# Moving attention's value products to the end of a unit, with a second pair of buffers for the turned weights

## The chip, the cores and the metric

The kernel runs on one NeuronCore of one Trainium2 chip, as one launch. The metric is the device time of that core in microseconds (us), as the median of several executions; smaller is better. The names of the engines are those of the profile: PE is TensorE's matmul, PEld its weight load, DVE is VectorE, ACT is ScalarE, POOL is GpSimd, SP is SyncE.

## The reference, cut to what matters

The reference is one inference step of a two-layer streaming encoder: 512 frames of a new stream (the prompt) and 32 next frames of a running stream (the sample) with 512 cached frames. Each layer projects the frames, runs three gated branches (convolution, spatial gating, stick-breaking attention), merges them, and ends with a feed-forward part. All in fp32. The change touches the attention alone:

```python
SB_HEADS = 8
SB_HEAD_DIM = BRANCH_W // SB_HEADS      # 64
SB_QBLOCK = 128

def stick_breaking(q, k, v, q_pos, k_pos):
    z = jnp.einsum('bqhd,bkhd->bhqk', q, k, preferred_element_type=jnp.float32) * (SB_HEAD_DIM ** -0.5)
    mask = k_pos[None, :] < q_pos[:, None]
    log_keep = jnp.where(mask, jax.nn.log_sigmoid(-z), 0.0)
    later = lax.cumsum(log_keep, axis=3, reverse=True) - log_keep
    attn = jnp.where(mask, jnp.exp(jax.nn.log_sigmoid(z) + later), 0.0)
    return jnp.einsum('bhqk,bkhd->bqhd', attn.astype(v.dtype), v)

def stick_breaking_prompt(q, k, v):
    outs = []
    for i in range(seq // SB_QBLOCK):
        lo, hi = i * SB_QBLOCK, (i + 1) * SB_QBLOCK
        outs.append(stick_breaking(q[:, lo:hi], k[:, :hi], v[:, :hi], pos[lo:hi], pos[:hi]))
    return jnp.concatenate(outs, axis=1)
```

So a block of 128 queries sees one to four blocks of 128 keys: its weights are 128, 256, 384 or 512 wide.

## The kernel before, in words

**The big products.** Nearly all of the time is TensorE multiplying fp32 weights that ScalarE and VectorE split into a high and a low part (`wh`, `wl`); each product takes three matmuls of 272 columns (`three`, L1563, L1568, L1569). A chunk of weights (`chunk`) serves four units (`unit`): a unit fills one PSUM bank `acc` with 8 x 3 = 24 matmuls. `chunk` calls `mid(b)` after the first 12 matmuls of unit b and `end(b)` after the last.

**Attention rides in these gaps.** In five chunks of each layer (20 units, u = 0 to 19) TensorE does attention's small matmuls in the middle of unit u (`within(u)`) and at its end (`behind(u)`). Attention comes in 18 steps. Steps 0 to 15 are for the prompt: step n has heads 2(n/4) and 2(n/4)+1 and query block n%4, so its weights are (n%4+1) x 128 wide. Steps 16 and 17 are for the sample. One step passes through the engines like this:

- `scores(n)` on TensorE, at the end of unit n, for both heads, into the banks `score0` and `score1` (L1637);
- `sigmoids(n)` on ScalarE, called from `before(n+1)`: `keep` and `beta` of each head from the scores (L528, L529; odd steps keep their `beta` in `gex`);
- masks on GpSimd (L449), two selections per head;
- `made(n)` on VectorE, called from `attend(n+1)`: a scan (L1047) and a product (L1050) per head;
- `turns(n, 0)` on TensorE in the middle of unit n+2 and `turns(n, 1)` at its end: the weights of head 0 and of head 1 are transposed into the one bank `turned` (L1664), and ScalarE copies each out of it into `att` (L546, in `turned`);
- `values(n)` on TensorE in the middle of unit n+3, ahead of `turns(n+1, 0)`: the products with `vtok` (L1685) for both heads into the one bank `small`;
- `out_rows(n)` on ScalarE (L560, from `within(n+3)`) copies the result's high part out of `small`, and `rows_lo(n)` on VectorE (L1073, from `attend(n+3)`) takes the low part. It raises `yc_full`, and `values(n+1)` waits for that, since it overwrites `small`.

**What sets the order.** Each engine runs its own list in order. On VectorE `attend(u)` first does `made(u-1)` and then `rows_lo(u-3)`; behind it come the splitting of weights (L897, L903) and the convolution's taps (L1103). On ScalarE a unit is `before(u)`, `within(u)`, in every fourth unit the splitting of weights `hi()` (L477, 1.9 us), the copy of the finished accumulator (L583 or L655), `behind(u)`. A wait is on a count: `Count` holds how often a semaphore has been raised by the program text so far, and `c.seen(sem)` is that number at the place where it is called. `turns` ends with `c.skip(att_full[s])`, which counts the copy that ScalarE will make of what was just turned, and `values` begins with

```python
                    for b in range(2):
                        pe.wait_ge(att_full[b], c.seen(att_full[b]))
                    pe.wait_ge(yc_full, c.prev(yc_full))
```

After the five chunks comes one for the gating branch, in which `within(20)` does the last values, and `turn_gv` turns tokens.

Of the kernel before, what the change touches and what calls it, by code (L numbers as in the profile page):

```python
# [8 lines left out]
ACT = mybir.ActivationFunctionType  # L9
AX_X = mybir.AxisListType.X  # L10

P = 128
D = 1024
SEQ = 512
DEC = 32
# [9 lines left out]
PAST = 512  # L25
DH = 64
# [11 lines left out]
T4 = CT * T * 4  # L38
# [73 lines left out]
def trunk(nc, adds, x_in, win, wbr, wout, wup, wdn, par_in, bc_in, sguw_in, kc_in, vc_in, gh_in, fh_in,  # L112
          y_out, k_out, v_out, glu_out, ffn_out, sgu_out):
    with ExitStack() as ctx:
# [9 lines left out]
        def sb(name, shape, dt=F32, at=None):  # L124
            size = 4
            for s in shape[1:]:
                size *= s
            off = at
            if at is None:
                off = top[0]  # L130
                top[0] += (size + 31) // 32 * 32
            return nc.alloc_sbuf_tensor_at(name, shape, dt, offset=off)
# [16 lines left out]
        S = top[0]  # L149
# [5 lines left out]
        M = top[0]  # L155
# [8 lines left out]
        C = top[0]  # L164
        cbuf = sb("cbuf", [P, 2, GEX - 2])
        F = top[0]
        assert F + 11 * T4 <= nc.sbuf_usable_end, F + 11 * T4

        wh.append(sb("wh3", [P, CHUNK], F32R, at=F + 79360))
        raw.append(sb("raw3", [P, CHUNK], at=F + 71168))  # L170
# [12 lines left out]
        vc = sb("vc", [P, CT, CH], at=F + 4 * T4 + CT * PAST * 4)  # L183
# [10 lines left out]
        keep = [sb(f"keep{i}", [P, T + 4], at=F + 90016 + i * 2208) for i in range(2)]  # L194
        beta = [[sb(f"beta0{i}", [P, T], at=C + i * 2176) for i in range(2)],
                [gex[:, i, 4:GEX] for i in range(2)]]
        att = [sb("att0", [P, 5 * P], at=S), sb("att1", [P, 5 * P], at=M)]
        sqc = [sb("sqc0", [P, CT, HALF], at=F + 90016), sb("sqc1", [P, CT, HALF], at=F + 71168)]

        cst = [st0[:, :], cbuf[:, 0, 0:HALF]]  # L200
# [6 lines left out]
        bt = ctx.enter_context(nc.psum_tensor("turned", [P, 512], F32))  # L207
# [89 lines left out]
        STEPS = 16  # L297
        ALL = STEPS + 2
# [166 lines left out]
        def _(act):  # L465
# [75 lines left out]
            def turned(n, part):  # L541

                act.wait_ge(t_full, c.take(t_full))
                if n < STEPS:
                    w = (n % 4 + 1) * P
                    A(att[part][:, 0:w], bt[:, 0:w], ACT.Copy).then_inc(att_full[part], c.up(att_full[part]))  # L546
                elif part == 0:
                    s = n - STEPS
                    A(att[s][:, 0:PAST], bt[:, 0:PAST], ACT.Copy).then_inc(att_full[s], c.up(att_full[s]))
                else:  # L550
                    s = n - STEPS
                    A(att[s][0:DEC, PAST:PAST + P], bt[0:DEC, 0:P], ACT.Copy).then_inc(att_full[s], c.up(att_full[s]))

            def out_rows(n):

                if n == STEPS:
                    return
                act.wait_ge(o_full, c.take(o_full))
                if n < STEPS:
                    A(yc[0][:, n // 4, n % 4 * P:(n % 4 + 1) * P], bo[:, 0:P], ACT.Copy).then_inc(o_hi, c.up(o_hi))  # L560
                else:
                    A(yc[0][:, :, SEQ:T], bo[:, 0:P].rearrange("p (a n) -> p a n", a=CT), ACT.Copy).then_inc(
                        o_hi, c.up(o_hi))

            def before(n):
                if 1 <= n <= ALL:
                    sigmoids(n - 1)

            def within(n):
                if 3 <= n < ALL + 3:  # L570
                    out_rows(n - 3)
                if 2 <= n < ALL + 2:
                    turned(n - 2, 0)

# [4 lines left out]
            def plain(dst, m, b, sig_to, fn=ACT.Copy):  # L579

                h = b // 2
                act.wait_ge(acc_full[b], c.take(acc_full[b]))
                A(dst[:, m, dcol(h)], ps[b][:, 0:HALF], fn).then_inc(acc_free[b], c.up(acc_free[b]))  # L583
# [20 lines left out]
            for l in range(DEPTH):  # L604
# [87 lines left out]
                    act.wait_ge(acc_free[b], c.seen(acc_free[b]))  # L692
                A(gv[:, 0:2, :], gv[:, 0:2, :], ACT.Gelu)
                A(gv[:, 2:4, :], gv[:, 2:4, :], ACT.Gelu).then_inc(gelu_v, c.up(gelu_v))
                within(STEPS + 4)
                hi()
                for b in range(4):
                    plain(gu, 2 + b % 2, b, None, ACT.Gelu)
                A(gu[:, 0:2, :], gu[:, 0:2, :], ACT.Gelu).then_inc(gelu_u, c.up(gelu_u))

                def token_root():
# [172 lines left out]
        def _(dve):  # L874
# [38 lines left out]
            def lo():  # L913

                if turn[0] == len(SIZES):
                    return
                s, n = SLOT[turn[0]], SIZES[turn[0]]
                turn[0] += 1
                dve.wait_ge(hi_full[s], c.take(hi_full[s]))
                v.tensor_tensor(wl[s][:, 0:n], raw[s][:, 0:n], wh[s][:, 0:n].bitcast(F32),  # L920
                                ALU.subtract).then_inc(lo_full[s], c.up(lo_full[s]))
# [144 lines left out]
            def rows_lo(n):  # L1066

                if n == STEPS:
                    return
                dve.wait_ge(o_hi, c.take(o_hi))  # L1070
                if n < STEPS:
                    ht, cols = n // 4, slice(n % 4 * P, (n % 4 + 1) * P)
                    v.tensor_tensor(yc[1][:, ht, cols], bo[:, 0:P], yc[0][:, ht, cols].bitcast(F32),  # L1073
                                    ALU.subtract).then_inc(yc_full, c.up(yc_full))
                else:
                    v.tensor_tensor(yc[1][:, :, SEQ:T], bo[:, 0:P].rearrange("p (a n) -> p a n", a=CT),
                                    yc[0][:, :, SEQ:T].bitcast(F32), ALU.subtract).then_inc(yc_full, c.up(yc_full))

            def attend(n):
                if 1 <= n <= ALL:  # L1080
                    made(n - 1)
                if 3 <= n < ALL + 3:
                    rows_lo(n - 3)

            tapped = [0] * CT
            tap_end = [None] * CT
# [31 lines left out]
            for l in range(DEPTH):  # L1118
# [99 lines left out]
                def turned_gate(t):  # L1218
                    dve.wait_ge(tok_turned, c.take(tok_turned))
                    w = P if t < 4 else DEC  # L1220
                    v.tensor_copy(ntok[0:w, t, :], bt[0:w, :]).then_inc(tok_full, c.up(tok_full))
                    dve.wait_ge(tok_full, c.seen(tok_full))
                    v.bn_stats(bnst[0:w, t, :], ntok[0:w, t, :]).then_inc(vec, c.up(vec))
                    dve.wait_ge(vec, c.seen(vec))
                    v.bn_aggr(mv[0:w, t, :], bnst[0:w, t, :]).then_inc(vec, c.up(vec))

                skip(range(4))
                attend(STEPS + 4)
                lo()
                turned_gate(0)  # L1230
                turned_gate(1)
                taps(TAPS_UV)
# [312 lines left out]
        def _(pe):  # L1545
# [46 lines left out]
            def chunk(xs=(xh, xl), nk=KT, first=None, mid=None, end=None):  # L1592
                s = arrived()
                for b in range(4):
                    unit(s, b, b % 2, xs, nk, first and (lambda t, b=b: first(t, b)), mid and (lambda b=b: mid(b)),
                         done=b == 3)
                    if end:
                        end(b)
# [76 lines left out]
            def values(n):  # L1675

                if n < STEPS:
# [3 lines that stand above are left out]
                    ht, i = n // 4, n % 4  # L1681
                    for kb in range(i + 1):
                        for b in range(2):
                            h = 2 * ht + b
                            last = mm(bo[DH * b:DH * b + DH, 0:P], vtok[:, kb, h * DH:(h + 1) * DH],  # L1685
                                      att[b][:, kb * P:(kb + 1) * P], start=kb == 0, stop=kb == i)
                    last.then_inc(o_full, c.up(o_full))
                    return
                s = n - STEPS
                pe.wait_ge(att_full[s], c.seen(att_full[s]))  # L1690
                if s == 0:
                    pe.wait_ge(yc_full, c.prev(yc_full))
                for ht in range(CT):
                    h = 2 * ht + s
                    out = bo[DH * s:DH * s + DH, ht * DEC:(ht + 1) * DEC]
                    for kb in range(4):
                        mm(out, vc[:, kb, h * DH:(h + 1) * DH], att[s][:, kb * P + ht * DEC:kb * P + (ht + 1) * DEC],  # L1697
                           start=kb == 0, stop=False)
                    last = mm(out, vtok[0:DEC, 4, h * DH:(h + 1) * DH],
                              att[s][0:DEC, PAST + ht * DEC:PAST + (ht + 1) * DEC], start=False, stop=True)  # L1700
                if s == 1:
                    last.then_inc(o_full, c.up(o_full))

            def within(n):
                if 3 <= n < ALL + 3:
                    values(n - 3)
                if 2 <= n < ALL + 2:
                    turns(n - 2, 0)

            def behind(n):  # L1710
                if 2 <= n < ALL + 2:
                    turns(n - 2, 1)
                if n < ALL:
                    scores(n)

# [10 lines left out]
            for r in range(DEPTH):  # L1726
# [83 lines left out]
                            turn_tokens(gv, t, tok_turned, tok_full)  # L1810
                    return after

                chunk(mid=lambda b: within(STEPS + 4) if b == 0 else None, end=turn_gv(0))

                def mix(tiles):
                    if tiles[0] == 0:
# [181 lines left out]
```

## Time and profile before

| | before |
|---|---|
| median of 3 runs | 1827.33 us |
| lowest and highest | 1826.01 and 1827.64 us |
| the profiled execution's own time | 1829.25 us |
| its span in the profile | 1827.5 us |
| PE busy in it | 1801.4 us (99%) |
| DVE busy | 1138.7 us (62%) |
| ACT busy | 770.3 us (42%) |
| POOL busy | 85.8 us (5%) |
| mean granted TensorE clock | 0.996 of full speed |

The span runs from the first instruction to the last; the execution's own time is a little longer, as it holds what lies around the span. Attention's scores stand between 114 and 204 us of the span in layer 0 and between 1015 and 1105 us in layer 1. A matmul's row in the timeline shows its start and the time until its result is out; matmuls overlap, so the pace is read from start to start (about 0.125 us for one of 272 columns).

### The profile page before, as it was taken

To read this page: it belongs to the slowest core of one execution; us is meant where nothing else is said; L and a number is where in the kernel's file an instruction comes from. 1 tells how busy PE (TensorE), PEld (TensorE's weight loads), DVE (VectorE), ACT (ScalarE), POOL (GpSimd) and SP (SyncE) were. 2 spreads that over 40 slices of the span, in tenths; PEclk is the share of its full clock that TensorE was granted. 3 is DMA by queue.
4 is the path that set the end of the run, shared out by engine and by line. 5 is a ranking of instruction groups with operands and counts; after the bars stand their busy time and mean duration, and the time that the engine had idled before them with its cause. 6 is when DMAs were issued, how large, how long until landed. Compare 5 with 4: busy or idle time off the path is not lost.

```text
span 1827.5 us, 32837 instructions
## 1 busy us (share of the span) xinstructions
PE 1801.4 (99%) x14328; PEld 1758.3 (96%) x14328; DVE 1138.7 (62%) x1742; ACT 770.3 (42%) x1216; POOL 85.8 (5%) x155
## 2 busy tenths in 40 slices
PE   7999999999999999999999999999999999999997
PEld 7998899999999999999999889999999999999996
DVE  4788677664774444446667886776557644445565
ACT  3246432353454444434542564333544544443342
POOL 0023100000000000000000340000001000000000
PEclk9999999999999999999999999999999999999998
DMA  4531122222212222255525211222232222222543
GB/s 169 171 113 48 36 79 85 82 93 81 105 70 93 93 93 81 77 171 173 173 96 190 71 62 44 72 84 91 82 127 70 73 90 93 93 88 95 183 161 126
DMA packets 36368, 186.02 MB, mean 102 GB/s; under 512 B 7360, under 2 KB 11712, under 8 KB 17920
## 3 DMA queue, kind: packets, MB, share of 16 engines
q1 hardware_dynamic: 34560, 178.34, 28.8%
q10 hardware_dynamic: 1664, 5.57, 0.8%
q8 instruction: 113, 1.85, 0.4%
q14 instruction: 31, 0.25, 0.0%
HBM read 176.75 MB, written 7.15 MB: 101 GB/s over the span
## 4 chain that ended last, share of the span: by engine, by line
PE 95%; DVE 3%; DMA 1%; ACT 1%; issue 1%; ACTq 0%; DVEq 0%
PE acc L1563 29%; PE acc L1568 29%; PE acc L1569 29%; PE score L1637 1%; PE small L1685 1%; PE turned L1664 1%; DVE wl L920 1%; DMA xT<-x_in 1%; PE score L1569 1%; PE score L1568 1%; PE score L1563 1%; PE small L1697 1%; PE turned L1721 0%; PE score L1829 0%; ACT wh L477 0%
## 5 line engine op out<-in xcount | busy, mean ns | idle before, releaser
L1563 PE MATMUL acc<-xh,wh 128*128 128x272 f32 x2944 | 860.1, 292 | 10.7 <-DVE xl L880 8.2
L1568 PE MATMUL acc<-xl,wh 128*128 128x272 f32 x2944 | 849.7, 289 | 0.0
L1569 PE MATMUL acc<-xh,wl 128*128 128x272 f32 x2944 | 849.2, 288 | 0.0
L1563 PEld LDWEIGHTS acc<-xh,wh 128*128 128x128 f32 x2944 | 556.9, 189 | 26.4 <-issue 15.7
L1568 PEld LDWEIGHTS acc<-xl,wh 128*128 128x128 f32 x2944 | 556.6, 189 | 0.1
L1569 PEld LDWEIGHTS acc<-xh,wl 128*128 128x128 f32 x2944 | 555.4, 189 | 0.0
L920 DVE TENSOR_TENSOR wl<-raw,wh 128x2048 fp32r<-128x2048 f32 (+1 forms) x155 | 320.7, 2069 | 206.9 <-ACT wh L477 206.2
L477 ACT ACTIVATE wh<-raw 128x2048 fp32r<-128x2048 f32 (+2 forms) x175 | 306.8, 1753 | 158.0 <-DMA raw<-wdn 112.9
L1563 PE MATMUL acc<-fhh,wh 128*128 128x272 f32 x704 | 204.8, 291 | 1.7 <-DVE wl L920 1.7
L1569 PE MATMUL acc<-fhh,wl 128*128 128x272 f32 x704 | 202.5, 288 | 0.0
L1568 PE MATMUL acc<-fll,wh 128*128 128x272 f32 x704 | 202.4, 288 | 0.0
L1103 DVE SCALAR_TENSOR_TENSOR acc<-glu,par,acc 128x574 f32<-128x574 f32 x240 | 180.8, 814 | 0.1
L1435 DVE SCALAR_TENSOR_TENSOR cbuf<-gex,par,cbuf 128x546 f32<-128x546 f32 x44 | 34.5, 785 | 198.0 <-ACT cbuf L808 198.0
L1563 PEld LDWEIGHTS acc<-fhh,wh 128*128 128x128 f32 x704 | 132.5, 188 | 3.4 <-DVE wl L920 3.0
L1568 PEld LDWEIGHTS acc<-fll,wh 128*128 128x128 f32 x704 | 132.4, 188 | 0.2
L1569 PEld LDWEIGHTS acc<-fhh,wl 128*128 128x128 f32 x704 | 132.4, 188 | 0.0
L714 ACT ACTIVATE tmp<-acc,par 128x272 f32<-128x272 f32 x96 | 46.7, 488 | 197.6 <-PE acc L1569 197.5
L1563 PE MATMUL acc<-mh,wh 128*128 128x272 f32 x256 | 74.9, 292 | 0.0
L1047 DVE TENSOR_TENSOR_SCAN keep<-keep,zero 128x128 f32<-128x128 f32 (+4 forms) x68 | 58.9, 866 | 25.4 <-POOL beta L449 16.9
L1568 PE MATMUL acc<-ml,wh 128*128 128x272 f32 x256 | 73.8, 288 | 0.0
L1569 PE MATMUL acc<-mh,wl 128*128 128x272 f32 x256 | 73.5, 287 | 0.0
L817 ACT ACTIVATE fhh<-tmp 128x272 fp32r<-128x272 f32 x88 | 35.2, 430 | 81.9 <-DVE tmp L1463 42.2
(237 smaller groups left out, 2236.8 us busy)
## 6 DMA issues: line engine op xcount, KB each, us to landing
raw<-win SPq DMA_DIRECT2D x51, 1024.0 KB, 4.9
raw<-wup SPq DMA_DIRECT2D x44, 1024.0 KB, 4.9
raw<-wdn SPq DMA_DIRECT2D x32, 1024.0 KB, 4.9
raw<-wbr SPq DMA_DIRECT2D x24, 512.0 KB, 3.6
raw<-wdn SPq DMA_DIRECT2D x16, 768.0 KB, 4.2
raw<-wout SPq DMA_DIRECT2D x8, 1024.0 KB, 4.9
v_out<-vfm ACTq DMA_DIRECT2D x2, 1088.0 KB, 9.0
k_out<-k ACTq DMA_DIRECT2D x2, 1088.0 KB, 4.7
```

The lines of the kernel that those rows point to most:

```text
L477: A(wh[s][:, 0:n], raw[s][:, 0:n], ACT.Copy).then_inc(hi_full[s], c.up(hi_full[s]))
L714: A(tmp[:, b, :], ps[b][:, 0:HALF], ACT.Sigmoid, bias=col(par, PAR["b_gate"] + 8 * BRANCHES[n] + 2 * i + b % 2)).then_inc(acc_free[b], c.u ...
L817: A(row(fhh[b // 2], 2 * i + b % 2, 0, HALF), tmp[:, b, :], ACT.Copy).then_inc(f_hi, c.up(f_hi))
L920: v.tensor_tensor(wl[s][:, 0:n], raw[s][:, 0:n], wh[s][:, 0:n].bitcast(F32), ALU.subtract).then_inc(lo_full[s], c.up(lo_full[s]))
L1047: v.tensor_tensor_scan(keep[b][:, T - w:T][:, ::-1], keep[b][:, T - w:T][:, ::-1], zero[:, 0:1].broadcast_to([P, w]), 1.0, ALU.mult, ALU.a ...
L1103: v.scalar_tensor_tensor(out=acc[:, m, :], in0=glu_at(m, j), scalar=w, in1=acc[:, m, :], op0=ALU.mult, op1=ALU.add).then_inc(vec, c.up(vec))
L1435: v.scalar_tensor_tensor(out=cbuf[:, m, :], in0=gex[:, m, 1:GEX - 1], scalar=col(par, PAR["fw"] + FT + t), in1=cbuf[:, m, :], op0=ALU.mult ...
L1563: first = mm(out, a, xs[0], start=start, stop=False)
L1568: mm(out, a, xs[1], start=False, stop=False)
L1569: return mm(out, b, xs[0], start=False, stop=stop)
L1637: mm(bs[b][:, 0:w], q[rows, ht, i * P:w], k[rows, ht, 0:w], start=True, stop=True).then_inc(s_full[b], c.up(s_full[b]))
L1664: last = pe.transpose(bt[:, kb * P:(kb + 1) * P], beta[n % 2][part][:, kb * P:(kb + 1) * P], ident[:, :])
```

## The change

`values(n)` leaves the middle of unit n+3 (`within`) and goes to its end (`behind`), between `turns(n+1, 1)` and `scores(n+3)`. By then ScalarE has copied the weights of step n+1 out of the bank, so `att` gets a second pair of buffers, and steps take them in turn (`n % 2`). `out_rows(n)` moves on ScalarE from `within(n+3)` to the head of `before(n+4)`, ahead of the sigmoids of step n+3; `rows_lo(n)` moves on VectorE from `attend(n+3)` to `attend(n+4)`, behind `made(n+3)`. The last values (step 17) go from the middle to the end of the first unit of the gating chunk, ahead of the first turn of tokens. The waits in the bodies of `turns`, `values` and `scores` stay as they are. The core of the diff:

```diff
-        att = [sb("att0", [P, 5 * P], at=S), sb("att1", [P, 5 * P], at=M)]
+        att = [[sb("att00", [P, 5 * P], at=S), sb("att01", [P, 5 * P], at=F + 90016 + 2 * 2208)],
+               [sb("att10", [P, 4 * P], at=M), sb("att11", [P, 4 * P], at=M + 4 * P * 4)]]
...
-                    A(att[part][:, 0:w], bt[:, 0:w], ACT.Copy).then_inc(att_full[part], c.up(att_full[part]))
+                    A(att[n % 2][part][:, 0:w], bt[:, 0:w], ACT.Copy).then_inc(att_full[part], c.up(att_full[part]))
...
             def before(n):
+                if 4 <= n < ALL + 4:
+                    out_rows(n - 4)
                 if 1 <= n <= ALL:
                     sigmoids(n - 1)
 
             def within(n):
-                if 3 <= n < ALL + 3:
-                    out_rows(n - 3)
                 if 2 <= n < ALL + 2:
                     turned(n - 2, 0)
...
-                within(STEPS + 4)
+                before(STEPS + 4)
                 hi()
                 for b in range(4):
                     plain(gu, 2 + b % 2, b, None, ACT.Gelu)
+                    if b == 0:
+                        before(STEPS + 5)
...
             def attend(n):
                 if 1 <= n <= ALL:
                     made(n - 1)
-                if 3 <= n < ALL + 3:
-                    rows_lo(n - 3)
+                if 4 <= n < ALL + 4:
+                    rows_lo(n - 4)
...
                 lo()
+                attend(STEPS + 5)
...
             def within(n):
+                if 2 <= n < ALL + 2:
+                    turns(n - 2, 0)
+
+            def behind(n):
+
+                if 2 <= n < ALL + 2:
+                    turns(n - 2, 1)
                 if 3 <= n < ALL + 3:
                     values(n - 3)
-                if 2 <= n < ALL + 2:
-                    turns(n - 2, 0)
-
-            def behind(n):
-                if 2 <= n < ALL + 2:
-                    turns(n - 2, 1)
                 if n < ALL:
                     scores(n)
...
-                chunk(mid=lambda b: within(STEPS + 4) if b == 0 else None, end=turn_gv(0))
+                def last_values(b):
+                    if b == 0:
+                        behind(STEPS + 4)
+                    turn_first(b)
+
+                turn_first = turn_gv(0)
+                chunk(end=last_values)
```

How it moves TensorE's instructions, in unit 8 of layer 0, the one whose scores are those of step 8. The names `att_114` to `att_117` are the buffers of `att`, `beta_113` is `beta` of head 1, and what stands in brackets are the semaphores waited for. Before, from the last big matmul of the unit's first half on, and again from the last one of its second half on:

```order
L1569 MATMUL acc<-xh,wl_59 128x272
L1685 MATMUL small<-att_114,vtok 64x128 [waits yc_full,att_full1,att_full0]
L1685 MATMUL small<-att_115,vtok 64x128
L1685 MATMUL small<-att_114,vtok 64x128
L1685 MATMUL small<-att_115,vtok 64x128
L1664 MATMUL turned<-ident,beta_112 128x128 [waits att_full1,at_full0]
L1664 MATMUL turned<-ident,beta_112 128x128 x2
...
L1569 MATMUL acc<-xh,wl_59 128x272
L1664 MATMUL turned<-ident,beta_113 128x128 [waits att_full0,at_full1]
L1664 MATMUL turned<-ident,beta_113 128x128 x2
L1637 MATMUL score<-k,q 128x128 [waits acc_free1,acc_free2,acc_free0,acc_free3,sig_full1,sig_full0]
L1637 MATMUL score<-k,q 128x128
```

And after the change, the same two places:

```order
L1574 MATMUL acc<-xh,wl_59 128x272
L1669 MATMUL turned<-ident,beta_112 128x128 [waits att_full1,at_full0]
L1669 MATMUL turned<-ident,beta_112 128x128 x2
...
L1574 MATMUL acc<-xh,wl_59 128x272
L1669 MATMUL turned<-ident,beta_113 128x128 [waits att_full0,at_full1]
L1669 MATMUL turned<-ident,beta_113 128x128 x2
L1690 MATMUL small<-att_116,vtok 64x128 [waits yc_full,att_full1,att_full0]
L1690 MATMUL small<-att_117,vtok 64x128
L1690 MATMUL small<-att_116,vtok 64x128
L1690 MATMUL small<-att_117,vtok 64x128
L1642 MATMUL score<-k,q 128x128 [waits acc_free1,acc_free2,acc_free0,acc_free3,sig_full1,sig_full0]
```

The four value products, with their wait, have moved behind the second turn and directly ahead of the scores.

ScalarE's list from the copy of the first turned head in unit 9 to the sigmoids of step 9, before:

```order
L560 ACTIVATE ych<-small 128x128 [waits o_full]
L546 ACTIVATE att_114<-turned 128x512 [waits t_full]
L583 ACTIVATE gv<-acc 128x272 [waits acc_full1]
L546 ACTIVATE att_115<-turned 128x512 [waits t_full]
L528 ACTIVATE keep_110<-score 128x256 [waits at_full0,s_full0]
L529 ACTIVATE gex<-score 128x256
```

and after:

```order
L548 ACTIVATE att_116<-turned 128x512 [waits t_full]
L585 ACTIVATE gv<-acc 128x272 [waits acc_full1]
L548 ACTIVATE att_117<-turned 128x512 [waits t_full]
L562 ACTIVATE ych<-small 128x128 [waits o_full]
L530 ACTIVATE keep_110<-score 128x256 [waits at_full0,s_full0]
L531 ACTIVATE gex<-score 128x256
```

The copy out of `small` has moved from ahead of the first turned head to behind the second one, ahead of the sigmoids.

## Rows read from the trace of the kernel before

**Rows 1.** The page: busy time of each engine.

```profile
PE 1801.4 (99%) x14328; PEld 1758.3 (96%) x14328; DVE 1138.7 (62%) x1742; ACT 770.3 (42%) x1216; POOL 85.8 (5%) x155
```

**Rows 2.** What TensorE waited for, the largest: us in total, times, longest.

```profile
PE acc L1563 <- DVE xl L880: 8.2, 2, 7.4
```

**Rows 3.** Timeline of PE, 148 to 154 us: start, length, instruction [idle before].

```profile
148.28 1.13 PE L1637 MATMUL score<-k,q 64*128 64x512 f32 x4
...
150.82 0.29 PE L1569 MATMUL acc<-xh,wl 128*128 128x272 f32 x1
151.04 0.66 PE L1685 MATMUL small<-att,vtok 128*64 128x128 f32 x8
151.62 0.55 PE L1664 MATMUL turned<-ident,beta 128*128 128x128 f32 x3
...
153.40 0.29 PE L1569 MATMUL acc<-xh,wl 128*128 128x272 f32 x1
153.53 0.49 PE L1664 MATMUL turned<-ident,beta 128*128 128x128 f32 x3
153.94 0.49 PE L1637 MATMUL score<-k,q 64*128 64x128 f32 x4
```

**Rows 4.** Timeline of PE, 156 to 170 us, attention's own instructions.

```profile
156.08 0.88 PE L1685 MATMUL small<-att,vtok 128*64 128x128 f32 x12
...
158.89 0.60 PE L1664 MATMUL turned<-ident,gex 128*128 128x128 f32 x4
159.42 0.70 PE L1637 MATMUL score<-k,q 64*128 64x256 f32 x4
161.75 1.09 PE L1685 MATMUL small<-att,vtok 128*64 128x128 f32 x16
...
164.45 0.27 PE L1664 MATMUL turned<-ident,beta 128*128 128x128 f32 x1
164.65 0.92 PE L1637 MATMUL score<-k,q 64*128 64x384 f32 x4
167.19 0.44 PE L1685 MATMUL small<-att,vtok 128*64 128x128 f32 x4
...
169.66 1.13 PE L1637 MATMUL score<-k,q 64*128 64x512 f32 x4
```

**Rows 5.** Timeline of DVE, 151 to 171 us.

```profile
151.31 1.23 DVE L1047 TENSOR_TENSOR_SCAN keep<-keep,zero 128x512 f32<-128x512 f32 x1 [0.43 <-POOL gex L449]
...
155.31 0.28 DVE L1073 TENSOR_TENSOR ycl<-small,ych 128x128 fp32r<-128x128 f32 x1
...
164.34 0.28 DVE L1073 TENSOR_TENSOR ycl<-small,ych 128x128 fp32r<-128x128 f32 x1
...
170.39 0.28 DVE L1073 TENSOR_TENSOR ycl<-small,ych 128x128 fp32r<-128x128 f32 x1
```

**Rows 6.** Timeline of ACT: copies of the second turned head in two units.

```profile
154.67 0.50 ACT L546 ACTIVATE att<-turned 128x384 f32<-128x384 f32 x1
...
159.52 0.60 ACT L546 ACTIVATE att<-turned 128x512 f32<-128x512 f32 x1
```

**Rows 7.** Timeline of PE and DVE: a pair without, and with a wait for VectorE.

```profile
487.35 0.62 PE L1606 MATMUL small<-st,mean_d 128*128 128x272 f32 x2
...
1813.27 0.44 DVE L1000 TENSOR_TENSOR st<-st,xT 128x272 f32<-128x272 f32 x1
...
1813.76 0.73 PE L1606 MATMUL small<-st,mean_d 128*128 128x272 f32 x2 [1.01 <-DVE st L1000]
```

**Rows 8.** Timeline of POOL: one selection beside busy VectorE, one beside idle.

```profile
161.32 0.80 POOL L449 TENSOR_SCALAR_AFFINE_SELECT gex<-gex 128x128 f32<-128x128 f32 x1
...
166.86 0.29 POOL L449 TENSOR_SCALAR_AFFINE_SELECT beta<-beta 128x128 f32<-128x128 f32 x1
```

**Rows 9.** Windows: stretch, length, PE busy (x), PEld, DVE, ACT, POOL, PEclk, DMA, GB/s.

```profile
210.00:214.00 4.00, 4.00 (x47) 3.52 (x46) 0.00 (x0) 0.00 (x0) 0.00 (x0) 1.00 0.00 0
214.00:217.00 3.00, 3.00 (x16) 3.00 (x15) 0.00 (x0) 0.60 (x1) 0.00 (x0) 0.50 0.00 0
```

More of the change, by code:

```diff
@@ L166, in trunk @@
         F = top[0]
-        assert F + 11 * T4 <= nc.sbuf_usable_end, F + 11 * T4
+        assert F + 90016 + 2 * 2208 + 5 * P * 4 <= nc.sbuf_usable_end
         wh.append(sb("wh3", [P, CHUNK], F32R, at=F + 79360))
@@ L545, in turned @@
                     w = (n % 4 + 1) * P
-                    A(att[part][:, 0:w], bt[:, 0:w], ACT.Copy).then_inc(att_full[part], c.up(att_full[part]))
+                    A(att[n % 2][part][:, 0:w], bt[:, 0:w], ACT.Copy).then_inc(att_full[part], c.up(att_full[part]))
                 elif part == 0:
                     s = n - STEPS
-                    A(att[s][:, 0:PAST], bt[:, 0:PAST], ACT.Copy).then_inc(att_full[s], c.up(att_full[s]))
+                    A(att[0][s][:, 0:PAST], bt[:, 0:PAST], ACT.Copy).then_inc(att_full[s], c.up(att_full[s]))
                 else:
                     s = n - STEPS
-                    A(att[s][0:DEC, PAST:PAST + P], bt[0:DEC, 0:P], ACT.Copy).then_inc(att_full[s], c.up(att_full[s]))
+                    A(att[0][s][0:DEC, PAST:PAST + P], bt[0:DEC, 0:P], ACT.Copy).then_inc(att_full[s], c.up(att_full[s]))
             def out_rows(n):
@@ L1685, in values @@
                             last = mm(bo[DH * b:DH * b + DH, 0:P], vtok[:, kb, h * DH:(h + 1) * DH],
-                                      att[b][:, kb * P:(kb + 1) * P], start=kb == 0, stop=kb == i)
+                                      att[n % 2][b][:, kb * P:(kb + 1) * P], start=kb == 0, stop=kb == i)
                     last.then_inc(o_full, c.up(o_full))
@@ L1696, in values @@
                     for kb in range(4):
-                        mm(out, vc[:, kb, h * DH:(h + 1) * DH], att[s][:, kb * P + ht * DEC:kb * P + (ht + 1) * DEC],
+                        mm(out, vc[:, kb, h * DH:(h + 1) * DH], att[0][s][:, kb * P + ht * DEC:kb * P + (ht + 1) * DEC],
                            start=kb == 0, stop=False)
                     last = mm(out, vtok[0:DEC, 4, h * DH:(h + 1) * DH],
-                              att[s][0:DEC, PAST + ht * DEC:PAST + (ht + 1) * DEC], start=False, stop=True)
+                              att[0][s][0:DEC, PAST + ht * DEC:PAST + (ht + 1) * DEC], start=False, stop=True)
                 if s == 1:
@@ L1704, in within @@
             def within(n):
-                if 3 <= n < ALL + 3:
-                    values(n - 3)
                 if 2 <= n < ALL + 2:
@@ L1712, in behind @@
                     turns(n - 2, 1)
+                if 3 <= n < ALL + 3:
+                    values(n - 3)
                 if n < ALL:
```

## The prediction

> **What bounds the kernel now.** I read the page first: TensorE is busy 99% of the span [rows 1]. Then the list of what it waited for: its largest entry, 8.2 us, lies at the start of the program [rows 2], and no row of it names a line of attention. So while attention runs, the time is the length of TensorE's own list, and every other engine is hidden. I then read TensorE's timeline from start to start [rows 3, 4], and last VectorE's, ScalarE's and GpSimd's beside it [rows 5, 6, 8], to see by how much each is early: this change moves waits, so their slack decides.
>
> **What the change takes off TensorE's list.** Before a value product, the last big matmul stands 0.22 us ahead of it (150.82 to 151.04), before a turn only 0.13 (153.40 to 153.53) [rows 3]: a step of 0.09. Behind the last value product come 0.20 us until the turn: a lone small matmul's row is 0.27 long (the turn at 164.45) [rows 4], so in a row of 0.66 the last product starts 0.39 after the first, and the turn starts 0.58 after it [rows 3]. Three turns take 0.55 behind values and 0.49 behind a big matmul, 0.06 more [rows 3]. All of this (0.09 + 0.20 + 0.06 = 0.35, and the products themselves) leaves the middle of a unit. At its end stands now turn, values, scores in place of turn, scores. Turn to scores costs 0.20 (153.53 to 153.94 is 0.41, and the last of the three turns starts 0.49 - 0.27 = 0.22 after the first) [rows 3]; turn to values and values to scores are not in the trace; bounds are 0.13, the step from a big matmul to a turn, and 0.22, the one to a value product. I take 0.20 for each, the row of the like step, since both also change the shape of the weights (128x128, 128x64, 64x128). So 0.20 + 0.20 - 0.20 = 0.20 comes back, and a unit is shorter by 0.15 us (between 0.11 and 0.29 by the bounds). There are 15 such units in a layer (those with turns, values and scores); the last three units lose about 0.1 us together, since there the values stand alone anyway. Sum: 2 x (15 x 0.15 - 0.1) = **4.3 us less**, were nothing waited for. The trace thus shows a cost for every change of shape. The Trainium skill says the same (TensorEngine Tiling (Array Packing), Key Properties): a change of tiling mode drains TensorE. By that rule alone, four changes in a unit become three and the kernel gets faster; that is the first rival below.
>
> **What it does to the waits.** Two waits of `values` change their meaning.
>
> (a) The bank `small`. `values(n)` waits for `rows_lo(n-1)`, which VectorE now does in `attend(n+3)` behind `made(n+2)`, and that begins with the scores of step n+2, at the end of the unit before. Scores to free bank had one and a half units; now it has one. I call C the time from the start of scores to the end of that step's VectorE work, the L1073 row. For 512 wide: 148.28 [rows 3] to 155.31 + 0.28 = 155.59 [rows 5], C = 7.3. For 256 wide: 159.42 [rows 4] to 164.62, C = 5.2. For 384 wide: 164.65 to 170.67, C = 6.0. This is a chain of sigmoids, selections, scans and products in which VectorE itself waits for GpSimd (0.43 us before the scan at 151.31) [rows 5], so it doesn't shrink when TensorE waits. One part does: a selection took 0.80 us beside VectorE's taps and 0.29 beside an idle VectorE [rows 8]; in the 256 wide step the taps will be done earlier, and I take 5.0. For 128 wide the rows' 5.3 hold ScalarE and VectorE being late from splitting weights; both would be done by then, and I take under 4.5.
>
> (b) The copy of the second turned head. `values` waits for `att_full[1]` at the count seen where it is called. It is now called behind `turns(n+1, 1)`, which has just counted its own copy. So TensorE turns, and must wait until ScalarE has copied that same turn, though the products don't read it. Turn to end of copy: 158.89 [rows 4] to 159.52 + 0.60 = 160.12 [rows 6], 1.23 us for 512 wide; 1.64 for 384 wide (153.53 to 154.67 + 0.50), where ScalarE is late from splitting weights [rows 3, 6].
>
> Against both stands D, from the start of scores to where the next unit's values could start if nothing waited. It is the distance of two scores' starts less what left the middle (length of the values' row, less 0.07 for its tail, plus 0.15). Behind 512 wide: 153.94 - 148.28 - 0.74 = 4.92 [rows 3]. Behind 128: 159.42 - 153.94 - 0.96 = 4.52. Behind 256: 5.23 - 1.17 = 4.06. Behind 384: 5.01 - 0.52 = 4.49 [rows 3, 4]. When TensorE does wait, its start comes 0.05 after the other engine's end (1813.27 + 0.44 to 1813.76), and the first pair is 0.1 longer (0.73 against 0.62) [rows 7], so 0.15 on top. The stall in each unit:
> - behind 512 wide, bank: 7.3 + 0.15 - 4.92 = 2.5 us, 4 times in a layer;
> - behind 384 wide, bank: 6.0 + 0.15 - 4.49 = 1.7, 3 times;
> - behind 256 wide, bank: 5.0 + 0.15 - 4.06 = 1.1 (1.3 by the row), 3 times;
> - behind 128 wide, copy: turn at 158.89 - 153.94 - 0.96 = 3.99, + 1.23 + 0.15 - 4.52 = 0.85, 3 times (the bank would give 0.9 at most);
> - the first values (no bank to wait for) and the two units of the sample's first turns: copy alone, about 0.75 each by the same working, 3 times.
>
> Sum of a layer: 10.0 + 5.1 + 3.3 + 2.6 + 2.3 = 23.3; both layers 46.6. Nothing gives it back: behind the waiting values stand the scores, so the next chain starts late as well, and TensorE has no slack elsewhere.
>
> **What costs nothing.** ScalarE's `out_rows` now stands ahead of the sigmoids. It waits for values that end before the scores do, and its 0.28 us runs while the scores do. The second pair of `att` buffers adds no instruction and no transfer. SP's and GpSimd's lists stay as they are. The last values of a layer go behind the middle of a unit that waits for ScalarE's GELU anyhow; at most some tenths of a us either way.
>
> **The sum.** 46.6 - 4.3 = 42.3 us more. The profiled execution took 1829.25 us and its span 1827.5, the median is 1827.33, so the terms, read in one execution, hold for the median too: **1869.6 us**. A difference under 0.2% (3.7 us) could not be told from no change.
>
> **The rivals.**
> 1. *Faster: the waits are met in time.* If the bank and the copy were free whenever values come, only the list's shortening stays: 1827.3 - 4.3 = 1823.0 us. It decides if C stays below D in every unit; the rows have C above D by 0.9 to 2.4. For it speaks only that the chain's parts beside each other (selections, taps) could part. Chance 0.05.
> 2. *The bank's chain shortens, the copy alone binds.* With copies ending 1.64 and 1.23 us behind the turn, and some 0.8 for the narrow ones, the stalls are 1.4, 0.7, 0.7 and 0.85 us by width: 5.6 + 2.1 + 2.1 + 2.6 + 2.3 = 14.7 in a layer, 29.4 - 4.3 = 25 more: 1852 us. Against it: scans and products of a 512 wide step are 2 x (1.2 + 0.7) us by themselves. Chance 0.08.
> 3. *The change does not do what it says, the copy's wait.* If `values` waited only for the copies it reads, (b) falls away: 2 x (10.0 + 5.1 + 3.3) - 4.3 = 32.5 more, 1860 us. The program text speaks against it. Chance 0.05.
> 4. *The granted clock falls too.* Behind the sample's values, thin products of 32 columns that fill most of 210 to 214 us, the clock went to 0.5 (1.2 GHz) and TensorE started 16 matmuls in 3 us instead of 24 [rows 9], 1.0 us lost there and about 0.5 in the rest of that stretch. If each of the eight 2.5 us stalls did the same, 8 x 1.5 = 12 more: 1882 us. Against it: these stalls are shorter than that stretch, and dense matmuls stand on both sides; some of the eight may do it. The Trainium skill (TensorE: Matmul & The Clock Gate, Part 1) has the half clock as the state after idleness and full clock after activity; it would side with this rival. Chance 0.14.
>
> **How the numbers follow.** The forecast's own case has 0.68. It spans 1861 (the 512 wide chain 0.3 shorter, two clock falls of before gone, narrow units at their lower ends) to 1876 (256 wide by its row, stalls 0.3 longer, three clock falls). The range takes in rivals 3 and 4 and leaves out 1 and 2, 0.13 in all: 1857 to 1883. Faster: 0.05, rival 1. Within 0.2%: 0.02, taken from rival 2, whose chains could shorten until stalls and savings meet. Slower: the rest, 0.93.
>
> **What would show it.** In the profile after, TensorE's waits should have two new rows on the values' line: one on VectorE's `ycl` (20 times, some 37 us in total) and one on ScalarE's `att` (about 12 times, some 10 us). VectorE's and ScalarE's busy time stay within 1%. The middle of a unit should show big matmul to turn at 0.13 and no values. The distance of two scores' starts should be about 8.0 us behind 512 wide against 5.66, 6.2 behind 128 wide against 5.48. If values start without idle time behind the turns, (a) and (b) are both wrong; if the wait is there but shorter, C was mis-sized; if the clock's row shows more falls than before, rival 4 is at work.

## The result, and the profile after

| | before | after |
|---|---|---|
| median of 6 runs | 1827.12 us | 1878.08 us |
| lowest and highest | 1825.76 and 1827.64 us | 1875.58 and 1880.43 us |
| the profiled execution's own time | 1829.25 us | 1876.46 us |
| its span | 1827.5 us | 1874.7 us |
| mean granted TensorE clock in it | 0.996 | 0.988 |

The change makes the kernel slower: the ratio of after to before is 1.028, with a 95% interval from 1.0268 to 1.0291. That is 51.0 us more; the prediction said 42.3 more (1869.6 us, range 1857 to 1883).

The line numbers of the changed kernel are five higher on TensorE's lines of attention (L1642 scores, L1669 turns, L1690 values), four higher on VectorE's, two higher on ScalarE's. The page's busy times, against [rows 1]:

```profile
PE 1811.2 (97%) x14328; PEld 1770.1 (94%) x14328; DVE 1139.4 (61%) x1742; ACT 771.1 (41%) x1216; POOL 72.7 (4%) x155
```

The number of instructions is the same on every engine. TensorE's busy time rose by 9.8 us though it does the same work, since part of it now runs at the half clock (below): e_bank, which waits too but keeps the clock, has 1797.9 us. Its share fell: it now waits. GpSimd's fell by 13 us, 11.6 of them in attention's 128 selections; that they stand less often beside a busy VectorE would fit [rows 8], but was not tested. What TensorE waited for (us in total, times, longest), against [rows 2]; these are the four rows on the values' line and, for comparison, the one of before:

```profile
PE small L1690 <- DVE ycl L1077: 28.1, 18, 2.4
PE acc L1568 <- DVE xl L884: 7.6, 2, 7.4
PE small L1690 <- issue: 7.0, 10, 0.7
PE small L1690 <- ACT att L548: 2.4, 2, 1.2
...
PE small L1690 <- ACT att L554: 1.0, 2, 0.5
```

That is 38.5 us in 32 waits. `ycl` is the bank (`rows_lo`), `att` the copy of the turned head. The ten "issue" waits are copies too, though the profile names no releaser: the timeline below shows one that starts 0.09 us after the copy's end, and all ten are gone in e_copy, which takes the copy's wait out. TensorE's timeline over four units, attention's own instructions, against [rows 3, 4] (start, length, instruction, idle time before it):

```profile
163.60 0.49 PE L1642 MATMUL score<-k,q 64*128 64x128 f32 x4
...
167.59 0.60 PE L1669 MATMUL turned<-ident,gex 128*128 128x128 f32 x4
168.92 0.88 PE L1690 MATMUL small<-att,vtok 128*64 128x128 f32 x12 [0.73 <-issue]
169.73 0.70 PE L1642 MATMUL score<-k,q 64*128 64x256 f32 x4
...
174.52 1.09 PE L1690 MATMUL small<-att,vtok 128*64 128x128 f32 x16 [0.66 <-DVE ycl L1077]
175.54 0.92 PE L1642 MATMUL score<-k,q 64*128 64x384 f32 x4
...
181.71 0.44 PE L1690 MATMUL small<-att,vtok 128*64 128x128 f32 x4 [1.61 <-DVE ycl L1077]
182.08 1.13 PE L1642 MATMUL score<-k,q 64*128 64x512 f32 x4
...
189.47 0.66 PE L1690 MATMUL small<-att,vtok 128*64 128x128 f32 x8 [2.39 <-DVE ycl L1077]
190.06 0.49 PE L1642 MATMUL score<-k,q 64*128 64x128 f32 x4
```

All values stand behind a turn and ahead of scores, as the change says, and each group waits. The distances of two scores' starts, in stretches at the full clock:

| behind scores of width | before | forecast | after |
|---|---|---|---|
| 512 | 5.66 | 8.0 | 190.06 - 182.08 = 7.98 |
| 128 | 5.48 | 6.2 | 169.73 - 163.60 = 6.13 |
| 256 | 5.23 | 6.2 | 175.54 - 169.73 = 5.81 |
| 384 | 5.01 | 6.6 | 182.08 - 175.54 = 6.54 |

(The forecast's column is the old distance, less 0.15, plus the stall of the prediction.) VectorE's timeline beside it, against [rows 5], shows the bank's chain behind the 512 wide scores of 182.08:

```profile
185.03 1.23 DVE L1051 TENSOR_TENSOR_SCAN keep<-keep,zero 128x512 f32<-128x512 f32 x1 [2.02 <-POOL gex L451]
186.29 0.69 DVE L1054 TENSOR_TENSOR gex<-gex,keep 128x512 f32<-128x512 f32 x1
187.17 1.23 DVE L1051 TENSOR_TENSOR_SCAN keep<-keep,zero 128x512 f32<-128x512 f32 x1 [0.19 <-POOL gex L451]
188.43 0.69 DVE L1054 TENSOR_TENSOR gex<-gex,keep 128x512 f32<-128x512 f32 x1
189.04 0.28 DVE L1077 TENSOR_TENSOR ycl<-small,ych 128x128 fp32r<-128x128 f32 x1
```

Two scans and two products, then `rows_lo`, which ends at 189.32: 7.24 us after the scores' start. TensorE's values start at 189.47, 0.15 later. ScalarE's copies of the second turned head, against [rows 6]:

```profile
168.23 0.60 ACT L548 ACTIVATE att<-turned 128x512 f32<-128x512 f32 x1
...
174.08 0.27 ACT L548 ACTIVATE att<-turned 128x128 f32<-128x128 f32 x1
```

The first ends at 168.83, and the values that "waited for issue" start at 168.92. The second ends at 174.35, as good as together with the bank (`rows_lo`, at 174.09 + 0.28 = 174.37). The prediction's list of signs had 20 waits for `ycl` of 37 us and 12 for the copy of 10 us; here are 18 of 28.1 and 14 of 10.4. The 37 us were a sum of stalls by distances: each holds about 0.1 us beside the idle time, and the 256 wide term was too large. Two waits of 2.4 us changed sides, which is explained under the count in one execution.

### The profile page after: what moved, and what is told of

It reads as the page before. It is cut to its first block, busy times and chain, and to the rows that moved or that the text cites. A ratio compares the mean times of both kernels' runs of the same rounds, so it can differ in the third digit from the quotient of the medians.

```text
span 1874.7 us, 32837 instructions
## 1 busy us (share of the span) xinstructions
PE 1811.2 (97%) x14328; PEld 1770.1 (94%) x14328; DVE 1139.4 (61%) x1742; ACT 771.1 (41%) x1216; POOL 72.7 (4%) x155
## 4 chain that ended last, share of the span: by engine, by line
PE 90%; DVE 4%; ACT 2%; issue 2%; POOL 1%; DMA 1%; ACTq 0%; POOLq 0%; DVEq 0%
PE acc L1568 28%; PE acc L1573 27%; PE acc L1574 27%; PE small L1690 1%; PE score L1642 1%; DVE keep L1051 1%; DVE wl L924 1%; POOL keep L451 1%; DMA xT<-x_in 1%; PE turned L1669 1%; PE score L1573 1%; PE score L1574 1%; PE score L1568 1%; PE turned L1727 1%; PE small L1702 0%
```

## The experiments

The theory: in the new place the values wait for the bank behind a whole step of VectorE, and for a copy that they don't read; both stalls lie on TensorE's list in full, while the order itself saves 0.15 us a unit. The half clock (a granted clock of 0.5, which is 1.2 GHz) lies behind what the forecast was short of. The rivals: the new order itself costs; only one of the waits does; the clock's falls have nothing to do with the stalls. Ratios are against the kernel before, run on the same chip (medians 1827.03 us for the first four, 1826.51 us for the last three).

**e_both: both waits taken out, the order kept.** On VectorE `rows_lo` goes ahead of `made`, and `turns` notes the count of each copy, for which `values` then waits:

```diff
             def attend(n):
-                if 1 <= n <= ALL:
-                    made(n - 1)
                 if 4 <= n < ALL + 4:
                     rows_lo(n - 4)
+                if 1 <= n <= ALL:
+                    made(n - 1)
...
                 c.skip(att_full[s])
                 turned_by[0] = att_full[s]
+                copied[n, part] = (att_full[s], c.seen(att_full[s]))
...
                     for b in range(2):
-                        pe.wait_ge(att_full[b], c.seen(att_full[b]))
+                        pe.wait_ge(*copied[n, b])
...
                 s = n - STEPS
-                pe.wait_ge(att_full[s], c.seen(att_full[s]))
+                pe.wait_ge(*copied[n, 1])
```

> The changed order on TensorE is kept, both waits are taken out: VectorE does rows_lo ahead of made, so that the bank is free as soon as ScalarE has copied it, and values waits for the count of the copies that it reads, not of those just turned. Theory (bank and copy are the whole stall, the order itself saves 0.15 us in 15 units of a layer): no wait on the values' line is left, each middle of a unit keeps the step of 0.13 us, and the time is 1827.1 - 4.3 = 1822.8 us, faster than before (1821.5 to 1824.5). Rival (part of the loss lies in TensorE's new order itself, by its changes of shape or by what it makes late): clearly above 1827 us with idle time that is still there behind the turns.

Measured: 1822.76 us, ratio 0.9977 (0.9968 to 0.9986). The costliest group of values in the list of lines (count | busy, mean ns | idle before) has no idle time left:

```profile
L1692 PE MATMUL small<-att,vtok 128*64 128x128 f32 x320 | 24.5, 283 | 0.0
```

And TensorE's timeline over one unit of the kind of [rows 3]:

```profile
147.39 1.13 PE L1643 MATMUL score<-k,q 64*128 64x512 f32 x4
150.06 0.49 PE L1670 MATMUL turned<-ident,beta 128*128 128x128 f32 x3
151.91 0.49 PE L1670 MATMUL turned<-ident,beta 128*128 128x128 f32 x3
152.32 0.66 PE L1692 MATMUL small<-att,vtok 128*64 128x128 f32 x8
152.91 0.49 PE L1643 MATMUL score<-k,q 64*128 64x128 f32 x4
```

From scores to scores it is 152.91 - 147.39 = 5.52 us against 5.66 before: 0.14 saved. Turn to values takes 0.41 less the turns' own 0.22, values to scores 0.59 less the products' own 0.39: 0.19 and 0.20, where the forecast took 0.20 for each. So the order alone is worth what was worked out, and all of the loss lies in the two waits and in what they bring. The rival of a cost in the order falls. This version beats both kernels.

**e_bank: only the bank's wait taken out** (the first piece of the diff above, alone).

> Only the bank's wait is taken out: rows_lo stands ahead of made on VectorE. Theory: the copy's wait is left, 0.6 to 0.8 us in each unit and about 1.4 us behind 512 wide scores, where ScalarE is late from splitting weights. In a layer 4 x 1.4 + 3 x 0.8 + 3 x 0.73 + 3 x 0.7 + 2.1 = 14.4 us, both layers 28.8, less 4.3: 1827.1 + 24.5 = 1852 us (1847 to 1857), and with stalls this short no more half-clock stretches than before. Rival (the copy costs nothing, the bank is all): 1823 us. Rival (the bank costs nothing): as the changed kernel, 1878 us.

Measured: 1850.36 us, ratio 1.013 (1.0116 to 1.0144). TensorE's waits on the values' line (waits, and timeline behind 512 wide scores):

```profile
PE small L1690 <- issue: 24.2, 30, 1.3
...
PE small L1690 <- ACT att L554: 1.0, 2, 0.5
...
157.79 0.66 PE L1690 MATMUL small<-att,vtok 128*64 128x128 f32 x8 [1.26 <-issue]
158.38 0.49 PE L1642 MATMUL score<-k,q 64*128 64x128 f32 x4
```

No wait for `ycl` is left, and 32 waits of 25.2 us in total are. With the 0.1 us by which a first pair behind a wait is longer, 25.2 + 3.2 - 4.3 = 24.1 more, and 23.3 were measured. The copy alone binds, as rival 2 of the prediction had it (1852). Both extreme rivals fall: neither wait costs nothing. The two costs do not add up (23.3 us here, 40.1 in e_copy below, 51.0 together): both waits stand at the same instruction, and the later one counts.

**e_copy: only the copy's wait taken out** (the other pieces of the diff).

> Only the copy's wait is taken out: values waits for the counts of the copies it reads; the bank is freed behind made as in the changed kernel. Theory: stalls behind 512, 384 and 256 wide scores stay (2.5, 1.7 and 0.7 us, since there the bank is as late as the copy or later), those behind 128 wide and at the ends of the sequence go. 2 x (4 x 2.5 + 3 x 1.7 + 3 x 0.7) - 4.3 = 30.1 us more than before: 1857 us, and with the half-clock stretches of the changed kernel, which the long stalls bring, some 10 us more: 1867 us (1858 to 1871). If the half clock had nothing to do with the long stalls: 1857 us.

Measured: 1867.16 us, ratio 1.0209 (1.0189 to 1.0229). Waits:

```profile
PE small L1692 <- DVE ycl L1077: 31.5, 20, 2.4
```

Twenty waits for the bank, as forecast (10 in a layer). 31.5 + 2.0 - 4.3 = 29 us account for 1856; the median is 11 us above that, and the profiled execution's mean clock was 0.989. So the surplus over the waits stays while the bank's long stalls stay, and it is gone in e_bank, whose stalls are 1.3 us at most and whose clock was 0.995. The four executions of e_copy go with their clocks, from 1859.77 us at 0.991 to 1868.33 at 0.989: how often the clock falls changes from one execution to the next.

**e_fill: the changed kernel, with work put into its long stalls.** What the filler writes is overwritten by the scores.

```diff
                     turns(n - 2, 1)
+                if 4 <= n <= STEPS and n % 4 == 0:
+                    for b in range(2):
+                        pe.wait_ge(sig_full[b], c.seen(sig_full[b]))
+                    for r in range(FILL):
+                        mm(bs[r % 2][:, 0:HALF], identr[:, :], xh[:, r % KT, dcol(0)], start=True, stop=True)
```

> The changed kernel with 16 more matmuls of 272 columns (about 2.0 us) ahead of the values' wait in the eight units behind 512 wide scores; they write junk into a score bank that the scores overwrite. The output is unchanged. Theory (the long stalls let the granted clock fall, and that is what lies between the forecast of 1869.6 us and the measured 1878.1): the filler lies within the stall and costs nothing, the clock stays up, and the time falls by 7 to 12 us to 1866 to 1871 us, with two half-clock stretches or so as in the kernel before. Rival (the clock's falls cost nothing, or come from something else): 1878 us as the changed kernel. If the filler is on the path (no stall there): 8 x 2.0 = 16 us more, 1894 us.

Measured: 1867.62 us, ratio 1.0224 (1.021 to 1.0238): 10.5 us less than the changed kernel, with 128 matmuls more. Timeline and waits:

```profile
132.18 2.25 PE L1722 MATMUL score<-xh,identr 128*128 128x272 f32 x16
134.81 0.66 PE L1691 MATMUL small<-att,vtok 128*64 128x128 f32 x8 [0.38 <-DVE ycl L1078]
...
PE small L1691 <- DVE ycl L1078: 16.5, 19, 1.7
```

The filler lies in the stall, and values start when the bank is free, as they do without it; scores to scores is 7.98 us here as well. The mean clock is 0.995. Windows of the changed kernel (stretch, length, PE busy (x), PEld, DVE, ACT, POOL, PEclk, DMA, GB/s) show what it took away:

```profile
182.00:186.00 4.00, 4.00 (x31) 3.17 (x28) 1.98 (x3) 3.04 (x7) 1.09 (x3) 1.00 0.34 88
187.00:189.40 2.40, 0.08 (x1) 0.00 (x0) 2.19 (x4) 1.23 (x3) 0.14 (x1) 1.00 0.28 116
...
190.50:193.90 3.40, 3.40 (x19) 3.40 (x17) 2.78 (x7) 0.79 (x4) 1.15 (x4) 0.54 0.01 2
```

And a long window of e_fill over about the same part of the program:

```profile
180.00:195.00 15.00, 13.78 (x114) 11.88 (x114) 11.47 (x17) 8.21 (x18) 3.38 (x8) 1.00 0.20 72
```

In the changed kernel TensorE is idle from 187.0 to 189.4, and the next 3.4 us run at 0.54 of the clock, with 19 matmuls. In e_fill the clock stays at 1.00. One fall between attention's scores is left in its trace, at 1100 to 1105, behind a 384 wide stall that holds no filler. The Trainium skill (TensorE: Matmul & The Clock Gate, Part 1) has idleness as what brings the half clock. This trace agrees in kind; by the page, idle stretches as short as these would not be enough, and here the measurement decides.

**e_mid: the values back in the middle, without waits.** From e_both:

```diff
             def within(n):
                 if 2 <= n < ALL + 2:
                     turns(n - 2, 0)
+                if 3 <= n < ALL + 3:
+                    values(n - 3)
 
             def behind(n):
 
                 if 2 <= n < ALL + 2:
                     turns(n - 2, 1)
-                if 3 <= n < ALL + 3:
-                    values(n - 3)
...
-                chunk(end=last_values)
+                chunk(mid=lambda b: within(STEPS + 4) if b == 0 else None, end=last_values)
```

> As e_both (no wait is left), but the values go back to the middle of the unit, behind the first turn there. Theory (what e_both gains is one change of shape less in a unit: the values share theirs with the scores): in the middle the steps are 0.13 + 0.20 + 0.20 = 0.53 us for big matmul to turn, turn to values, values to big matmul, against 0.22 + 0.20 + 0.06 + 0.03 = 0.51 in the kernel before, so the gain is gone: 1827.1 + 0.6 = 1827.7 us (1826.5 to 1829). Rival (the gain of e_both comes from taking the values out of the wait chain, from the earlier turn or from the second buffers, not from where the values stand): 1822.8 us, as e_both.

Measured: 1835.29 us, ratio 1.0049 (1.0035 to 1.0062): above both. My expectation that no wait is left was wrong:

```profile
PE small L1692 <- DVE ycl L1077: 5.6, 6, 1.0
...
157.28 0.60 PE L1670 MATMUL turned<-ident,gex 128*128 128x128 f32 x4
158.79 0.88 PE L1692 MATMUL small<-att,vtok 128*64 128x128 f32 x12 [0.91 <-DVE ycl L1077]
```

ScalarE's copy out of `small` now comes only behind the copy of the second turned head, and in every fourth unit that one is late from splitting weights; half a unit later TensorE wants the bank again. ScalarE's timeline:

```profile
153.10 1.91 ACT L479 ACTIVATE wh<-raw 128x2048 fp32r<-128x2048 f32 x1
155.08 0.40 ACT L585 ACTIVATE gv<-acc 128x272 f32<-128x272 f32 x1
155.37 0.48 ACT L548 ACTIVATE att<-turned 128x384 f32<-128x384 f32 x1
155.74 0.29 ACT L562 ACTIVATE ych<-small 128x128 fp32r<-128x128 f32 x1
```

The waits, with their longer first pairs, are 5.6 + 0.6 = 6.2 of the 8.8 us above before. The rest is 2.6, where 0.6 was expected; the units without a wait are 0.04 to 0.07 us longer than before (for instance 5.05 against 5.01 behind 384), which makes about 1.5 of it in 30 units. So the gain of e_both did vanish with the values' place, as the theory has it, and the rival's 1822.8 is excluded. But the run is not a clean count of changes of shape, since a wait came with it; what is left of about 1 us stays open.

**e_sfirst: scores ahead of the values.** From e_both:

```diff
-                if 3 <= n < ALL + 3:
-                    values(n - 3)
                 if n < ALL:
                     scores(n)
+                if 3 <= n < ALL + 3:
+                    values(n - 3)
```

> As e_both, but the scores stand ahead of the values at the end of the unit: turn, scores, values, big matmul. Theory: the changes of shape are three as in e_both, and nothing waits, so an earlier start of the scores gives nothing: 1822.8 us (1821.8 to 1824). Rival (ScalarE's or VectorE's chain still sets something): some us faster, since each chain starts 0.4 to 1.0 us earlier.

Measured: 1822.73 us, ratio 0.9978 (0.997 to 0.9987), the same as e_both. Without waits it doesn't matter when the chain starts; TensorE's list is the time again. The order turn, scores, values has three changes of shape as well.

**e_split: the sample's thin products in halves.** From e_both; each of the two steps does two of its four head pairs in the middle of the unit and two at its end:

```diff
             def within(n):
+                if n > STEPS + 2:
+                    values(n - 3, (0, 1))
                 if 2 <= n < ALL + 2:
                     turns(n - 2, 0)
...
                 if 3 <= n < ALL + 3:
-                    values(n - 3)
+                    values(n - 3, (2, 3) if n > STEPS + 2 else range(CT))
...
-                chunk(end=last_values)
+                chunk(mid=lambda b: within(STEPS + 4) if b == 0 else None, end=last_values)
```

> As e_both, but the 40 thin value products of each of the sample's two steps are split: 20 in the middle of the unit, 20 at its end. Theory (the clock fell behind them, twice per kernel, because they keep TensorE thinly loaded for 3.2 us at a stretch): no half-clock stretch is left in attention, which gives back 2 x 1.5 = 3.0 us, and four more interruptions at about 0.25 us cost 1.0: 1820.8 us (1820 to 1822.5), the fastest so far. Rival (the falls have another cause): 1823.8 us with the clock falling as before.

Measured: 1821.69 us, ratio 0.9973 (0.9962 to 0.9984); the mean clock is 0.997. The window behind the thin products, in e_both first and then the one around them in e_split:

```profile
213.40:216.40 3.00, 3.00 (x14) 2.94 (x14) 0.36 (x1) 2.61 (x2) 0.00 (x0) 0.50 0.33 90
```

```profile
212.00:215.00 3.00, 3.00 (x32) 2.84 (x32) 0.00 (x0) 2.97 (x5) 0.00 (x0) 1.00 0.11 12
```

In e_both 14 matmuls in 3 us at half the clock; in e_split the clock stays full there. TensorE is not idle ahead of these falls (busy 4.00 of 4.00 us in [rows 9]). The fall does not come each time: in the eight traces with undivided blocks it is there in 11 of 16 layers (in neither layer of e_copy, in one of e_fill, e_mid and e_sfirst). But all seven executions of e_split have a clock of 0.997, where e_both's eleven go from 1820.65 us at 0.997 to 1824.10 at 0.995. So it is the undivided block behind which the clock can fall, and the split avoids it. What that is worth is not resolved: the median is 1.1 us below e_both's, and the two intervals overlap.

## Why the prediction was right, point by point

- **The list (4.3 us less).** Right in size: e_both came out at 1822.76 us, where rival 1 of the prediction, which is the same kernel without waits, gave 1823.0. The two steps that the trace of before did not show were taken from their like, and measured 0.19 and 0.20. The Trainium skill's rule that a change of tiling mode drains TensorE (TensorEngine Tiling (Array Packing), Key Properties) agreed with the row, and would have misled whoever stopped there.
- **(a) The bank.** Right. Behind 512 wide scores C was 7.24 against 7.3, behind 384 wide the stall is 6.54 - 4.86 = 1.68 against 1.7. The mis-sized term is the 256 wide one: C was taken as 5.0 and came out as 174.37 - 169.73 = 4.64, and the stall as 5.81 - 5.08 = 0.73 against 1.1, some 2 us too much over six units. That the row's 5.2 held a selection beside busy taps was seen, but only partly taken off.
- **(b) The copy.** Right: 6.13 - 5.33 = 0.80 against 0.85 behind 128 wide. e_bank has it alone, at 23.3 us, e_copy takes it out.
- **The waits together.** The stalls by the full-clock distances are 2.47, 0.80, 0.73 and 1.68 us; 4 x 2.47 + 3 x (0.80 + 0.73 + 1.68) = 19.5, and some 2.0 at the ends of the sequence: 21.5 in a layer, 43 in both, where the prediction had 46.6. Less 4.3 that is 39 us more. The prediction's remark that the unit of the last values waits for ScalarE's GELU anyhow has no row behind it: no wait of TensorE in the trace of before names ScalarE.
- **The clock.** This is the step that was short. It stood as rival 4, at 0.14, and at nothing in the sum. 51.0 - 39 = 12 us lie there; e_fill takes 10.5 of them away (1878.08 to 1867.62, while the kernel before took 1827.12 and 1827.03 us beside them). The price of a fall was right (1.5 us forecast): in the changed kernel the unit that starts with the scores of 190.06 lasts 7.67 us, its like at 163.60 lasts 6.13. How often it falls was not: [rows 9] showed it behind thin products only, and nothing in the trace of before showed what a stall does. The mean clock of 0.988 and 0.996 over the spans says (1 - 0.988) x 2 x 1875 = 45 us at half the clock, against 15 before; some 11 and 9 of them lie at the program's end, where TensorE has nothing left to do.
- **The count in one execution.** The profiled execution of the changed kernel took 1876.46 - 1829.25 = 47.2 us more than that of before. Its waits give 38.5 + 3.2 - 4.3 = 37.4. The units in which the clock fell are together 9.7 us longer than their like at the full clock. The sum is 47.1. A fall right behind a 512 wide stall costs about 1.5 us (the one of 1140.09 lasts twice as long and costs 2.9). One behind a 384 wide stall costs 0.3 to 0.4, because the next stall takes up the rest: the unit of 155.34 lasts 8.26 us against 7.98, and its stall is 1.13 instead of 2.4. In that unit and one other the copy comes last and not the bank, hence 18 waits for `ycl` and not 20.
- **The number.** Two misses run against each other: the waits were 3.6 us too many, the clock 12 too few. That the range held owes something to this, and to its having been drawn around rival 4. The forecast's own case ended at 1876; the measured 1878.1 lies above it, and nearer to rival 4's 1882 than to 1869.6. The direction and both waits were right; the chances of the own case (0.68) and of rival 4 (0.14) were not well placed.
- **Rivals 1 to 3.** 1 and 2 came true only in e_both and e_bank, where the edits made them so, at 1822.8 and 1850.4 (1823.0 and 1852 forecast); 3 is e_copy without the clock's falls, and with them it is 1867.

## What to carry to other kernels

Before moving work on the bounding engine, measure for each of its waits the distance between the release and the use, and compare that with the move: here 0.15 us a unit was to be had, and a slack of one and a half units became one. A wait on a count that is taken where the code stands changes its meaning when the code is moved; note the count where the producer is issued. And the engine that frees a buffer should do so ahead of its long work: one reordering on VectorE and one exact count turned 51 us of loss into 4.3 us of gain.

## What the runs showed of the hardware that I had not expected

Stalls of 1.6 to 2.4 us between dense matmuls are enough for TensorE's clock to fall to half (1.2 GHz). In the changed kernel's windows TensorE is idle for most of 152.9 to 155.0, behind 384 wide scores, and from 156 to 159 the clock is at 0.61. The stall at the end of that unit is then the shorter one:

```profile
152.90:155.00 2.10, 0.37 (x5) 0.17 (x4) 2.07 (x5) 0.67 (x2) 0.00 (x0) 1.00 0.00 0
156.00:159.00 3.00, 3.00 (x16) 2.60 (x13) 0.97 (x2) 2.07 (x4) 0.83 (x3) 0.61 0.44 79
...
154.97 0.44 PE L1690 MATMUL small<-att,vtok 128*64 128x128 f32 x4 [1.73 <-DVE ycl L1077]
155.34 1.13 PE L1642 MATMUL score<-k,q 64*128 64x512 f32 x4
...
163.02 0.66 PE L1690 MATMUL small<-att,vtok 128*64 128x128 f32 x8 [1.13 <-ACT att L548]
```

But it does not fall behind each: the stall of 181.71 was followed by full clock (182 to 186 above). In the traces of the changed kernel and of e_copy it fell behind 11 of 13 stalls of 2.4 us and behind 3 of 12 of 1.6 to 1.7 us; in e_bank, with 1.3 us at most, behind none. What decides between two like stalls stays open. And matmuls put into a stall that stays as it is paid: 128 more of them made the kernel 10.5 us faster.
